# A per-slot table in device memory for the combine matrices of a mixture-of-experts kernel

## The reference

```python
def hierarchical_moe(x, ...):           # 4 groups of 8 experts, 512 hidden units each
    grp_p, grp_idx = top_k(softmax(xt @ w_rg + b_rg), 1)
    exp_p, exp_idx = top_k(softmax(logits of the group's experts), 2)
    gates = grp_p * exp_p / sum(exp_p)
    # every token goes through its two experts:
    #   (silu(x @ w_gate[e]) * (x @ w_up[e])) @ w_down[e], times its gate
    x = x + hierarchical_moe(rms_norm(x, ln_ffn[layer]), ...)
```

## Time and profile before

| | |
|---|---|
| median of 3 runs | 1741.19 us (1739.01 to 1742.21) |
| the profiled execution's own time | 1740.96 us |
| its span in the trace | 1739.2 us |
| PE busy | 1708.6 us, 98% of the span |
| DVE, ACT, POOL busy | 654.3, 444.9, 215.5 us |
| DMA traffic | 460.39 MB, mean 265 GB/s |
| the two mixtures, pairs | about 335 to 812 us and 1253 to 1730 us |

### The profile page before, as it was taken

The page is one execution under the profiler, slowest core; times in us unless marked ns, Lnnn a source line. Parts: engine busy times, 40 slices in busy tenths (PEclk is TensorE's granted clock), DMA queues, the critical chain, the costliest instruction groups (busy, mean ns, idle before and its releaser), DMA issues.

```text
span 1739.2 us, 23472 instructions
## 1 busy us (share of the span) xinstructions
PE 1708.6 (98%) x9323; PEld 1102.6 (63%) x9323; DVE 654.3 (38%) x1164; ACT 444.9 (26%) x868; POOL 215.5 (12%) x152
## 2 busy tenths in 40 slices
PE   7999999999999999999999999999999999999998
PEld 6888988654545444455888888888654544545453
DVE  3865863422323323234414123132522332323233
ACT  4565653211111111112332323213311111111110
POOL 1500000100000000001543343442000000000000
PEclk9999999999999999999999999999999999999999
DMA  9410112699999999997122122122499999999995
GB/s 199 102 49 1 50 50 98 264 429 411 424 418 420 414 422 415 415 424 269 51 96 97 49 97 97 60 93 90 194 417 414 423 414 418 423 413 422 413 420 216
DMA packets 67449, 460.39 MB, mean 265 GB/s; under 512 B 5552, under 2 KB 31376, under 8 KB 41904
## 3 DMA queue, kind: packets, MB, share of 16 engines
q1 hardware_dynamic: 66640, 457.01, 65.0%
q0 software_dynamic: 736, 2.34, 1.2%
HBM read 457.24 MB, written 2.10 MB: 264 GB/s over the span
## 4 chain that ended last, share of the span: by engine, by line
PE 96%; DVE 2%; ACT 1%; issue 1%; DMA 0%; SPq 0%; DVEq 0%; ACTq 0%
PE bank L153 31%; PE bank L1725 25%; PE bank L1736 13%; PE bank L1743 7%; PE bank L1696 7%; PE bank L1701 2%; PE bank L2248 1%; PE bank L1730 1%; PE bank L1491 1%; PE bank L1710 1%; PE bank L940 1%; PE bank L927 1%; PE bank L515 1%; PE bank L943 0%; PE bank L868 0%
## 5 line engine op out<-in xcount | busy, mean ns | idle before, releaser
L1725 PE MATMUL bank<-ring,SCR 128*64 128x512 f32 x2048 | 445.0, 592 | 0.9 <-DVE SCR L1705 0.9
L153 PE MATMUL bank<-ring_r 128*128 128x512 f32 (+2 forms) x1216 | 359.1, 377 | 5.2 <-DVE ring_r L400 2.4
L1725 PEld LDWEIGHTS bank<-ring,SCR 128*64 128x64 f32 x2048 | 148.7, 137 | 290.8 <-issue 290.8
L153 PEld LDWEIGHTS bank<-ring_r 128*128 128x128 f32 x1216 | 225.5, 192 | 46.5 <-issue 4.1
L2179 POOL TENSOR_TENSOR ring_r<-ring,ring_r 128x1024 fp32r<-128x1024 f32 x62 | 150.8, 2468 | 698.5 <-ACT ring_r L2172 698.5
L1736 PE MATMUL bank<-ring,SCR 128*64 128x512 f32 x1024 | 226.8, 595 | 1.7 <-DVE X L2024 1.7
L2024 DVE TENSOR_TENSOR X<-X,bank 128x512 f32<-128x512 f32 x240 | 148.5, 681 | 97.3 <-PE bank L1743 97.2
L1755 DVE SCALAR_TENSOR_TENSOR SCR<-SCR,bank 128x512 f32<-128x512 f32 x32 | 23.9, 748 | 356.3 <-PE bank L1725 356.3
L1736 PEld LDWEIGHTS bank<-ring,SCR 128*64 128x64 f32 x1024 | 71.5, 137 | 133.2 <-issue 129.6
L153 PE MATMUL bank<-ring_r,SCR_r 128*128 128x512 f32 x576 | 138.7, 395 | 0.0
L1743 PE MATMUL bank<-SCR_r 128*128 128x512 f32 x512 | 131.5, 399 | 0.5 <-DVE SCR_r L1752 0.5
(11 more groups left out here) (413 smaller groups left out, 1699.5 us busy)
## 6 DMA issues: line engine op xcount, KB each, us to landing
ring<-in_w_gate_dram SPq DMA_DIRECT2D x64, 2048.0 KB, 12.7
ring<-in_w_up_dram SPq DMA_DIRECT2D x64, 2048.0 KB, 16.1
ring<-in_w_down_dram SPq DMA_DIRECT2D x64, 2048.0 KB, 12.1
ring<-in_w_in_odd_dram SPq DMA_DIRECT2D x8, 2048.0 KB, 8.9
ring<-in_w_in_even_dram SPq DMA_DIRECT2D x16, 512.0 KB, 6.8
ring<-in_w_in_odd_dram SPq DMA_DIRECT2D x8, 1024.0 KB, 8.0
ring<-in_w_out_odd_dram SPq DMA_DIRECT2D x4, 2048.0 KB, 7.9
ring<-in_w_out_even_dram SPq DMA_DIRECT2D x2, 2048.0 KB, 8.4
```

The costliest lines, as they stand in the source:

```text
L153: mm = pe.matmul(out, lhs[a], rhs[b], start=(first and i == 0), stop=(last and i == 2))
L1725: mm = pe.matmul(bank[SLOTS * u:SLOTS * u + SLOTS, :], x_tile(k, u), w[u][:, k, :], start=(k == 0), stop=(k == KT - 1))
```

## The change

From the second pair on, `OT` and `GSL` are no longer made by way of TensorE. After the routing VectorE works out for each token the two numbers (expert x 64 + place) of its slots (`slots_dve`); POOL writes token number and gate of each, 8 bytes, to a table in device memory at those numbers with eight indirect DMAs of 128 entries (`table_pool`), waits for them, and reads the table back (2048 entries of 8 bytes) into `TAB`, which has the 128 slots of a pair in the partitions and the 16 pairs in the columns. For each pair VectorE copies the gates' column and compares the token column with the numbers 0 to 511 (`ot_rows`). Pair 0 is done as before. The table starts at -1 and 0, written early in the kernel (`table_init`).

```diff
+    even["base"] = np.broadcast_to(SLOTS * np.arange(NE) - 1, (P, NE))
+    even["token"] = i[:, None] + P * np.arange(NT)[None, :]
...
+    slot_table = [nc.dram_tensor(f"slot_table{l}", (NE * SLOTS, 2), F32) for l in range(2)]
...
-            step(dve.tensor_tensor(by_group(M1), by_group(M1), per_group(go1), ALU.mult))
+            step(dve.tensor_tensor(by_group(GG), by_group(M1), per_group(go1), ALU.mult))
             step.then(dve.tensor_tensor(go2, ohg, bt(gate2), ALU.mult))
-            step.then(dve.tensor_tensor(by_group(M2), by_group(M2), per_group(go2), ALU.mult))
-            step(dve.tensor_tensor(GG, M1, M2, ALU.add))
+            step.then(dve.tensor_tensor(by_group(MG), by_group(M2), per_group(go2), ALU.mult))
+            step(dve.tensor_tensor(GG, GG, MG, ALU.add))
...
+        def slots_dve(dve, l, step):
+            by_group = lambda a: a.rearrange("p t (g e) -> p t g e", g=NG)
+            bounds = const("base")[:, None, :].to_broadcast([P, NT, NE])
+            step(dve.tensor_scalar(D2.rearrange("p t e -> p (t e)"), POSM.rearrange("p t e -> p (t e)"), float(SLOTS), 1.0e5, ALU.is_gt, ALU.mult))
+            step(dve.tensor_tensor(D1, POSM, bounds, ALU.add))
+            for c, gate in enumerate((gate1, gate2)):
+                step(dve.tensor_copy(entry[:, c, :, 0], const("token")))
+                step(dve.tensor_copy(entry[:, c, :, 1], gate))
+            step.wait()
+            step.then(dve.tensor_tensor(D1, D1, D2, ALU.add))
+            step.then(dve.tensor_tensor(by_group(D1), by_group(D1), ohg[:, :, :, None].to_broadcast([P, NT, NG, EPG]), ALU.mult))
+            step.then(dve.tensor_tensor(D2, D1, M1, ALU.mult))
+            step(dve.tensor_reduce(dest_f[:, 0, :], D2, AX, ALU.add))
+            step.then(dve.tensor_tensor(D1, D1, M2, ALU.mult))
+            step.then(dve.tensor_reduce(dest_f[:, 1, :], D1, AX, ALU.add))
+            dve.tensor_copy(dest[:, :, :], dest_f).then_inc(moe_sem(l, "dests"), 1)
+            dve.wait_ge(*moe_wait(l, "ot", 1))
+            step(dve.tensor_tensor(IOTA.rearrange("p (n s) -> p n s", s=SLOTS), const("slot")[:, None, :].to_broadcast([P, SEQ // SLOTS, SLOTS]),
+                                   const("base")[:, 0:SEQ // SLOTS, None].to_broadcast([P, SEQ // SLOTS, SLOTS]), ALU.add))
+            step.wait()
+
+        def table_init(pool, step):
+            step(pool.memset(TAB[:, :, 0], -1.0))
+            step.then(pool.memset(TAB[:, :, 1], 0.0))
+            for l in range(2):
+                pool.dma_start(slot_table[l][:, :].rearrange("(p i) v -> p i v", p=P), TAB[:, :, :]).then_inc(sg("table_clear"), 16)
+
+        def table_pool(pool, l):
+            pool.wait_ge(*moe_wait(l, "dests", 1))
+            pool.wait_ge(sg("table_clear"), 32)
+            for t in range(NT):
+                for c in range(2):
+                    pool.indirect_dma_start(slot_table[l][:, :], bass.IndirectOffsetOnAxis(ap=dest[:, c, t:t + 1], axis=0), entry[:, c, t, :], None,
+                                            bounds_check=NE * SLOTS - 1, oob_is_err=False).then_inc(sg("scattered"), 16)
+            pool.wait_ge(sg("scattered"), 16 * 2 * NT * (l + 1))
+            pool.dma_start(TAB[:, :, :], slot_table[l][:, :].rearrange("(i p) v -> p i v", p=P)).then_inc(sg("slots_in"), 16)
...
+        def ot_rows(dve, i, b):
+            pair = one(i)
+            dve.tensor_copy(GSL[:, b:b + 1], TAB[:, pair, 1])
+            return dve.tensor_tensor(OT[b], IOTA, TAB[:, pair, 0].to_broadcast([P, SEQ]), ALU.is_equal)
...
 (TensorE, pair)
                     x_transposed(i + 1, 0)
-                    slots_transposed(i + 1)
                     x_transposed(i + 1, 1)
                 down(i)
...
 (ScalarE, pair)
                     x_gathered(i + 1, 1)
-                    slot_gates(i + 1, 1 - b)
                 y_out(i)
...
 (VectorE, pair)
                 if more:
                     dve.wait_ge(*mw("gat", 2 * i + 2))
-                    dve.wait_ge(*mw("ohg", i + 1))
                     one_hots(i + 1).then_inc(ms("oh"), 1)
-                dve.wait_ge(*mw("gs_out", i + 1))
-                ot_ones(dve, b).then_inc(ms("ot_out"), 1)
-                if more:
-                    dve.wait_ge(*mw("oh", i + 2))
-                    dve.wait_ge(*mw("ot", i + 1))
-                    gated(i + 1).then_inc(ms("ohg"), 1)
+                if is_at(i, 0):
+                    dve.wait_ge(*mw("rexp", 4))
+                    ot_ones(dve, 0).then_inc(ms("ot_out"), 1)
+                else:
+                    if is_at(i, 1):
+                        dve.wait_ge(sg("slots_in"), 16 * (l + 1))
+                    else:
+                        dve.wait_ge(*mw("comb", 8 * i - 8))
+                    ot_rows(dve, i, b).then_inc(ms("ot_out"), 1)
                 hidden(i, b)
...
             x_out(0, 0)
             x_out(0, 1)
+            slots_dve(dve, l, step)
             pairs_loop(dve, pair)
...
 (POOL's queue)
             attn_pool(pool, step)
+            table_init(pool, step)
...
                 norm_pool(pool, 1, step)
+                table_pool(pool, 0)
                 pool.wait_ge(*moe_wait(0, "logits3", 1))
                 pool.dma_start(SCR[:, CO_AT:SCR_N], const_odd).then_inc(odd_in, 16)
...
                 norm_pool(pool, 3, step)
+                table_pool(pool, 1)
```

More of the change, by code:

```diff
@@ L1418, in program @@
         cnt = sb("cnt", [P, 1], I32)
-        ROUTE = dict(m_route_pe=("logits0", "logits1", "logits2", "logits3", "counts"), m_route_dve=("gain", "gdiff", "ediff", "masks", "oh_first", "routed"))
-        PER_LAYER = dict(rexp=3, xn_upper=NT, xn_lower=NT,
-                         **dict.fromkeys(("oh", "ohg", "ot", "ot_out", "gs_out", "gate", "up", "sil", "hh", "ht", "ht_out"), PAIRS),
+        IOTA = OHG.rearrange("p t n -> p (t n)")
+        TAB = sb("TAB", [P, PAIRS, 2])
+        dest_f = s_(2 * NT).rearrange("p (c t) -> p c t", c=2)
+        dest = sb("dest", [P, 2, NT], I32)
+        D1, D2 = (tg(AU[:, 400 + n * NT * NE:400 + (n + 1) * NT * NE]) for n in range(2))
+        entry = s_(4 * NT).rearrange("p (c t v) -> p c t v", c=2, t=NT)
+        ROUTE = dict(m_route_pe=("logits0", "logits1", "logits2", "logits3", "counts", "ot"), m_route_dve=("gain", "gdiff", "ediff", "masks", "oh_first", "routed", "ohg", "dests"))
+        PER_LAYER = dict(rexp=4, xn_upper=NT, xn_lower=NT,
+                         **dict.fromkeys(("oh", "ot_out", "gate", "up", "sil", "hh", "ht", "ht_out"), PAIRS),
                          **dict.fromkeys(("gat", "xg", "xt", "xt_out", "y", "y_upper", "y_lower"), NE),
@@ L1840, in x_transposed, with slots_transposed @@
                 xt_mm(pe, g).then_inc(ms("xt"), 1)
[L1842 to L1845, removed]
+            def slots_transposed():
+                pe.wait_ge(*mw("ohg", 1))
                 ot_mm(pe).then_inc(ms("ot"), 1)
@@ L1871, in experts_pe @@
             x_transposed(0, 1)
-            slots_transposed(0)
+            slots_transposed()
             pairs_loop(pe, pair)
@@ L1929, in x_gathered, with slot_gates @@
                 act.copy(XG[:, half * 512:(half + 1) * 512], BX[half][:, :]).then_inc(ms("xg"), 1)
[L1931 to L1935, removed]
+            def slot_gates():
+                act.wait_ge(*mw("ot", 1))
+                ot_gates(act, 0).then_inc(ms("rexp"), 1)
             def y_out(i):
@@ L1960, in experts_act @@
             x_gathered(0, 1)
-            slot_gates(0, 0)
+            slot_gates()
             pairs_loop(act, pair)
@@ L2008, in hidden @@
                 dve.wait_ge(*mw("sil", i + 1))
-                dve.wait_ge(*mw("gs_out", i + 1))
                 dve.wait_ge(*mw("up", i + 1))
+                dve.wait_ge(*mw("ot_out", i + 1))
                 hidden_mul(dve, b).then_inc(ms("hh"), 1)
```

## The result

The change made the kernel slower. Median of the kernel after: 1745.50 us (1741.48 to 1747.99, 9 runs); of the kernel before, on the same chip: 1741.54 us (1739.01 to 1743.10, 9 runs). The ratio is 1.0021, with a 95% interval of 1.0011 to 1.0030, so some 4 us. The forecast was 1730.8 us. The profiled execution took 1746.62 us, its span is 1744.8, 5.6 longer than before.

A forecast was written before the change was run, and what follows sets the result against it. TensorE was taken to set the pace of the pairs, with the DMA engines nearly full. Transposes removed, -13.2 us, plus a 2.8 us wait made -10.4 against 1740.96, so 1730.6, as a median 1730.8; range 1726.5 to 1741.

The forecast's parts named there:

- Part 1: Pairs 1 to 15 of each layer: slots' transposes leave TensorE's queue, 0.44 us each, 13.2 us gained in all.
- (c): Running pairs: the DMA engines become the bound, pairs not below 29.9 us; 1737.6, from 1734 to 1741; chance 0.12.
- (e): Pairs: each 0.44 us off TensorE returns as a wait for a piece or for additions; 1741; chance 0.03.
- Parts 2 and 3: VectorE and ScalarE work in each pair, and `slots_dve` once per layer (3.2 us): covered by waits, worth nothing.
- Part 4: Table on POOL's queue: 0.91 us per indirect DMA, read back by 367.9, needed by 378, 10 us to spare.
- Rival (d): Table late in each layer, indirect DMAs costing over 2.2 us each; at 4 us each, 1756; chance 0.13.
- Part 5: Extra and moved DMA work, 7.5 us in layer 0: TensorE waits 2.8 us once in pair 1 or 2; layer 1 none.
- The slack: `up` pieces landing before need: layer 0, 4.4 us in pair 1, 4.8 in pair 2; layer 1, 5.6.
- The load: Layer 0 DMA work: router loads 1.8, read-back 1.6, scatters 0.8 counted half, `const_odd` 3.7; layer 1, 2.4 at most.
- the moved loads: Layer 0, POOL's queue: `const_odd` (3.7 us) and layer 1's router loads (1.8) now fall among pieces for pairs 1 and 2.
- My upper bound: Wait for `up` in layer 0: at most 6.8 us, with 8-byte pieces at three times the router's price.

The follow-up runs named there:

- experiment 5: Kernel after without the eight indirect DMAs of each layer and the wait for them, read-back and moved loads kept: 1736.93 us, ratio 0.9965.
- experiment 4: Kernel after with layer 0's table stage put behind `const_odd` and the router loads on POOL's queue: 1742.34 us, ratio 1.0008.
- experiment 9: Kernel after padded to 64 columns, with 100000 added to each slot number so that the indirect DMAs write nothing: 1734.94 us, a single execution.
- experiment 1: Kernel before with 36 unused columns added to the constants, placing SCR as in the kernel after: 1745.15 us against 1740.81, ratio 1.0023.
- experiment 2: Kernel after with 28 unused columns more in the constants, 64 columns or 256 bytes in all: 1739.73 us, ratio 0.9997.
- experiment 3: Kernel before with 16 unused columns in the constants, moving SCR by 64 bytes: 1745.26 us in a single execution, against a median of 1741.43.
- experiment 6: Kernel before plus only `TAB` and the early clearing by `table_init`, the table never used: 1740.12 us, ratio 0.9988.
- experiment 8: Kernel before, transposes kept, plus the whole table traffic with its result unused and 28 unused columns for alignment: 1749.43 us, ratio 1.0051.
- experiment 7: Kernel after with 28 unused constant columns more and layer 0's table stage behind `const_odd` and the router loads: 1734.55 us, ratio 0.9958.
- experiment 10: Kernel after, padded and with the old load order, pairs 0 to 3 done the old way, five scatters behind TensorE milestones: 1732.78 us, ratio 0.9947.
- experiment 11: As experiment 10, but the table used from pair 2 on, four scatters at once and four at milestones: 1729.57 us, ratio 0.9937.

## Why the prediction was wrong

The time moved the other way, so the sum missed more than one term. In the order of the sum:

**Part 1, right but for the first pair.** In the running pairs the transposes left the chain and nothing else took their place. At a good place a pair fell from 30.15 to 29.72 us, against the predicted 29.71. Neither `down` nor the DMA engines hold the pairs: 29.72 goes on through both mixtures, so rivals (c), as a steady bound, and (e) did not occur. But pair 0 of each layer gained nothing. It has no combine, so TensorE reaches the transposes of the tokens while ScalarE still copies them out, and the slots' transpose had filled that wait. The chain of experiment 5:

```profile
356.50 1.89 PE bank L1737 x8
358.39 0.02 issue
358.41 0.59 ACT SCR L1972
359.01 0.04 issue
359.05 0.74 PE bank L1742 x4
359.80 7.02 PE bank L1782 x32
```

From the end of the gather to `down` it is 1.41 us; with the slots' transpose in between it was 1.43 in the kernel before (353.70 to 355.13), and the period of pair 0 is 26.6 us in both. So the prediction's 30 x 0.44 = 13.2 us are 28 x 0.43 = 12.0.

**Parts 2 and 3, right.** The slot numbers were there at 340.4, 2.6 us after the second `x_out` ended, against a sum of 3.2, and no wait of TensorE came of it.

**Part 4, right in its result, in part by luck.** An indirect DMA holds POOL for 0.97 us, 1.27 with the gap, where I took 0.91 and a limit of 2.2. VectorE got on at 367.85, against 367.9 in the prediction, because two errors cancel: the mixture began 2.5 us later than before, and the read-back landed in 8.6 us, quicker than the 10.2 that I took. VectorE waited for the table, and TensorE not for VectorE:

```profile
367.85 0.15 DVE L1767 COPY SCR<-TAB 128x1 f32<-128x1 f32 x1 [1.17 <-DMA TAB<-slot_table]
```

Rival (d) did not occur, though the time came out on its side.

**Part 5, the step that failed.** "TensorE waits 7.5 - 4.7 = 2.8 us in pair 1 or 2, once", and for layer 1 "no wait". The place was right: `up` in pair 1. The lag was 7.2 us in layer 0 and 2.2 in layer 1. Two terms had the wrong size, and one was missing.

The slack. The 14.8 us of the earlier trace rows is the median of two pieces that land 4.9 us apart, and I added only 0.4 for the second. Asked for each alone, the two of layer 0 and the second of layer 1 landed, in the kernel before, after

```profile
ring<-in_w_up_dram SPq DMA_DIRECT2D x1, 2048.0 KB, 12.6
ring<-in_w_up_dram SPq DMA_DIRECT2D x1, 2048.0 KB, 17.0
ring<-in_w_up_dram SPq DMA_DIRECT2D x1, 2048.0 KB, 16.0
```

and `up` waits for the later one. That is 366.8 against a need at 369.0: the slack was 2.2 us and not 4.4, for pair 2 2.5 and not 4.8 (the second piece landed at 396.2), in layer 1 3.1 and not 5.6 (1283.4).

The load. "Eight scatters (1024 pieces) 0.8, of which I count half": I turned the share of the engines that a queue of short pieces has the earlier trace rows into the time that it takes from the others. (Even that share was not all the router's: until 336.3 `const_odd` was landing on the same queue, and from there to 365 us the queue took 3.4% of 28.7 us, 1.0 us.) In layer 1, where nothing is moved, the second piece landed 4.5 us later than before (20.44 us after its issue, for 15.98), where I had 2.4 at most. In layer 0 it landed 6.6 us later (23.68 for 17.04), near the 7.5 of the sum, but by luck: with the moved loads at their old place (experiment 4) it is 21.27, so scatters and read-back took 4.2 us, where the sum has 2.0, and the moved loads 2.4, where it has 5.5. Experiments 5 and 9 name the scatters in layer 1; in layer 0 leaving out the writes takes 1.4 us off the lag and the old order 3.2 to 4.0, and the rest stays undivided.

The clock. The sum has no term for what a wait does to the matmuls behind it: 2.7 of the 7.2 us in layer 0 are `up` at the lower clock.

My upper bound, 8-byte pieces at three times the router's price, gave 6.8 us in layer 0 and 2.4 + 4.0 - 5.6 = 0.8 in layer 1, both too low. With the slack as it was it gives 9.2 and 3.3, and holds.

**The step that was missing: the place of the operands.** Nothing in the prediction asks what two constant tables do to the addresses behind them. Experiment 1 prices it at 4.3 us by its medians, and experiment 2 takes it back. It is as large as the error of part 5 in layer 0 (7.2 against 2.8, 4.4 us), and half of it falls in a stage that the change does not touch.

**The end.** From the end of the last addition to the end of the span it took 3.5 us in the kernel before and in experiments 1, 3, 6 and 8, 5.0 to 5.2 in the kernel after and in experiments 2, 4, 5, 7 and 9, and 4.7 and 4.1 in experiments 10 and 11. The DMA engines in the last 7 us of the kernel after:

```profile
GB/s 351 24 351 421 398 421 398 421 398 141 140 421 398 515 374 351 374 374 375 398 351 445 398 445 398 141 24 23 23 47 23 23 23 23 23 0 0 0 0 0
```

In its last 1.6 us the stores go on at only 23 GB/s, about what one of the 16 engines moves when all move 427. It is neither the place nor the table's traffic, since experiment 8 has both traffic and 3.5 us. What makes these last stores late stays open.

**The sum again.** By the milestones: -12.0 (28 periods), +2.3 (place, in the mixtures), +2.3 (place, between), +7.2 and +2.2 (`up`), +1.2 (the end) make +3.2 us. The span says +5.6, of which 2.5 lie ahead of the first mixture. That stage moves by itself: it ended between 333.1 and 340.0 us in these profiles, and the later the lower the granted clock had been from 150 to 262 us: 0.98 in experiment 7 (333.1), 0.97 in the kernel before (335.4), 0.94 in the kernel after (337.9), 0.92 in experiment 5 (340.0). Experiment 11, at 0.95, ended it at 335.2, so the clock doesn't explain all of it; what share the place has is open. The difference of the medians, +4.0, lies between the two.

## What to carry to other kernels

An edit that only adds a buffer moves all buffers behind it, and that alone can cost over a third of what the edit gains (4.6 of 12.0 us here): keep the buffers behind an addition where they were modulo 256 bytes a partition, as the padding did here, and compare stages that the edit does not touch before explaining those that it does. Where weights stream at the limit, many tiny writes to device memory are to be priced by what the stream loses beside them, not by their own share of the engines; issue them spread out, and as late as their reader allows. When an engine waits for several pieces, take its slack from the landing of the last one, not from their median. A gain that is right per step can still be lost whole at the start of a stage, where slack is smallest and where a step may have been hidden in a wait all along.

## What the runs showed of the hardware

- A matmul of 128x512 from `ring_r` with `SCR_r` took 390 ns with the constants at their old size or 256 bytes more, and 396 with 64 or 128 bytes more (first retention projections; 395 and 399 over the span). The gather shows it too: `XN_r,SCR_r`, 391 ns before (L1696) and 395 after (L1742).
- 1024 indirect writes of 8 bytes nearly stopped the weight stream twice in each layer, for 1.5 to 2 us each time, at 1% of the engines' time. With all entries dropped, and the same 1%, the weights kept moving.
- After TensorE had stood still for 4.55 us its granted clock was 0.50 in the stretch from 376 to 380 us, and 32 matmuls took 9.55 us in place of 6.87. After a wait of 1.33 us in layer 1 it stayed at 1.00.
- In the kernel after, an indirect DMA of 128 entries held POOL for 0.97 us, the first one for 1.47, with 0.30 us between two.
